# Two more U blocks per retrieval tile, thirty-six expert blocks on the spot, and one comparison for four one-hot rows

## The reference, cut to what matters

```
q = (xb @ wq).reshape(T, PEER_HEADS, 2, PEER_DKEY // 2)
s = jnp.einsum('thpk,hpnk->thpn', q, keys)
sv, si = lax.top_k(s, PEER_TOPK)                       # 16 of 128, per head and half
cand = sv[:, :, 0, :, None] + sv[:, :, 1, None, :]     # 16 x 16 sums
cv, ci = lax.top_k(cand, PEER_TOPK)
e = i1 * PEER_NKEYS + i2                               # 8 heads x 16 = 128 experts per token
gate = jax.nn.softmax(cv, axis=-1)
act = jax.nn.gelu(jnp.einsum('ted,td->te', u_tab[e], xb))
return jnp.einsum('te,ted->td', gate * act, v_tab[e])
```

## Time and profile before

| what | us |
|---|---|
| median of three runs | 4249.58 |
| lowest and highest run | 4244.55, 4253.15 |
| profiled execution | 4253.82 |
| its span, first to last instruction | 4252.2 |
| DVE busy in the span | 2870.1 (67%) |
| PE busy in the span | 3772.1 (89%) |

### The profile page before, as it was taken

One profiled execution on the slowest core, in us unless ns is written; L12 is line 12 of the kernel. 1 busy time (PEld: TensorE's weight loads), 2 busy tenths in 40 slices (PEclk: granted clock), 3 DMA queues, 4 the chain that ended last, 5 costly groups with the idle time before them and its releaser, 6 DMA issues. The chain is left out here.

```text
span 4252.2 us, 62663 instructions
## 1 busy us (share of the span) xinstructions
PE 3772.1 (89%) x21957; PEld 3272.0 (77%) x21957; DVE 2870.1 (67%) x7070; ACT 1065.8 (25%) x1921; POOL 1407.0 (33%) x1144
## 2 busy tenths in 40 slices
PE   4999899888798888888999899999999899999996
PEld 3999788876698888887888788887888566555665
DVE  3653334437211999999998599999999465555566
ACT  4443222224211222223333222222222111111112
POOL 0120244432100000000000355655564466666641
PEclk7999899999899999999999999999999999999998
DMA  4111211114221323333766688888887699999974
GB/s 160 35 47 47 76 49 56 65 44 155 102 90 47 122 96 113 108 98 110 184 173 179 232 306 311 312 312 304 312 308 268 267 376 380 361 366 358 375 287 156
DMA packets 464443, 823.68 MB, mean 194 GB/s; under 512 B 224352, under 2 KB 286048, under 8 KB 462432
## 3 DMA queue, kind: packets, MB, share of 16 engines
q0 software_dynamic: 120816, 444.13, 29.1%
q1 hardware_dynamic: 343408, 376.80, 26.4%
HBM read 708.89 MB, written 111.94 MB: 193 GB/s over the span
## 5 line engine op out<-in xcount | busy, mean ns | idle before, releaser
L2273 POOL DMA_INDIRECT stored_rows<-in_peer_v,peer_idx x384 | 398.0, 1036 | 117.7 <-issue 107.3
L2506 POOL DMA_INDIRECT peer_y<-in_peer_u_rows,experts_idxU x231 | 318.7, 1379 | 263.4 <-DVE peer_y L2595 182.3
L2385 PE MATMUL stored_pv<-peer_xh 128*128 128x512 f32 x912 | 374.1, 410 | 35.5 <-DVE peer_xl L2316 31.6
L1797 PE MATMUL topk_pu<-peer_xh,topk_Uh 128*128 128x384 f32 x864 | 303.0, 351 | 88.6 <-DVE topk_Ul L1784 88.6
L2386 PE MATMUL stored_pv<-peer_xl,peer_xh 128*128 128x512 f32 x912 | 359.3, 394 | 0.0
L2387 PE MATMUL stored_pv<-peer_xh,peer_xl 128*128 128x512 f32 x912 | 356.8, 391 | 0.0
L2339 DVE TENSOR_TENSOR peer_y<-peer_y,stored_pv 128x512 f32<-128x512 f32 x456 | 293.2, 682 | 44.5 <-PE stored_pv L2387 44.5
L2312 DVE TENSOR_TENSOR peer_xl<-stored_Vr,peer_xh 128x1024 fp32r<-128x1024 f32 x76 | 94.1, 1238 | 329.9 <-ACT peer_xh L2291 329.9
L2385 PEld LDWEIGHTS stored_pv<-peer_xh 128*128 128x128 f32 x912 | 171.8, 188 | 169.1 <-issue 55.8
L1798 PE MATMUL topk_pu<-peer_xl,topk_Uh 128*128 128x384 f32 x864 | 298.2, 345 | 0.0
L1799 PE MATMUL topk_pu<-peer_xh,topk_Ul 128*128 128x384 f32 x864 | 298.0, 345 | 0.0
(11 more groups left out here) (374 smaller groups left out, 9697.8 us busy)
## 6 DMA issues: line engine op xcount, KB each, us to landing
gates<-gates_G SPq DMA_DIRECT2D x48, 1024.0 KB, 11.3
stored_Vr<-in_peer_v SPq DMA_DIRECT2D x76, 512.0 KB
stored_C<-acts SPq DMA_DIRECT2D x76, 384.0 KB, 6.5
stored_G<-gates SPq DMA_DIRECT2D x76, 384.0 KB, 8.5
topk_Ur<-in_peer_u SPq DMA_DIRECT2D x56, 512.0 KB, 3.7
experts_Ur<-in_peer_u SPq DMA_DIRECT2D x52, 512.0 KB, 7.3
experts_Vr<-in_peer_v SPq DMA_DIRECT2D x52, 512.0 KB, 8.4
acts<-topk_act SPq DMA_DIRECT2D x108, 192.0 KB, 1.9
```

Source lines behind the costliest of these rows:

```text
L1797: mm(dst, self.Uh[slot][:, k, :], self.xh[:, k, cols], start=(k == 0), stop=False)
L2273: pool.indirect_dma_start(buffer(g, j), None, dram["peer_v"].rearrange("a b d -> (a b) d"), bass.IndirectOffsetOnAxis(idx[:, n:n + 1], 0)) ...
L2385: mm(pv[r % RING][:], Ch[p][j][:, t], Vh[p][j][:, cols], start=(j == 0), stop=False)
L2506: pool.indirect_dma_start(ug[i], None, dram["peer_u_rows"], bass.IndirectOffsetOnAxis(which, 0)).then_inc(ug_in[i], 16)
```

## The change

Retrieval makes eight U blocks per tile with a ring of four slots (72 instead of 54), the extra blocks behind the gates are two instead of four, so `MADE` is 92 instead of 76. The stage on the spot has 36 blocks (18 pairs instead of 26), the stored stage 92 (46 pairs instead of 38). `PER` becomes 23 instead of 16. In the gates one tensor_tensor of 128 x 512 makes the four `one` rows of a bank; the `scaled` rows stay as they are.

```diff
-TOPK_AHEAD, TOPK_RING = 6, 3
+TOPK_AHEAD, TOPK_RING = 8, 4
 GATE_AHEAD, GATE_RING = 3, 3
-EXTRA = 4
+EXTRA = 2
 MADE = TILES * TOPK_AHEAD + DENSE * GATE_AHEAD + EXTRA
...
                     dve.wait_ge(used, t * BANKS + (b + 1))
+                    four = core.slotT[:, 2, bass.ds(t * P + (FIRST + b * TG), TG)].unsqueeze(2).to_broadcast([P, TG, P])
+                    nc.vector.tensor_tensor(one[i][:], iota[:].unsqueeze(1).to_broadcast([P, TG, P]), four, ALU.is_equal)
                     for j in range(TG):
                         slot = lambda which: core.slotT[:, which, bass.ds(t * P + (FIRST + b * TG + j), 1)]
-                        nc.vector.tensor_scalar(one[i][:, j, :], iota[:], slot(2), None, ALU.is_equal)
                         last = nc.vector.tensor_scalar(scaled[i][:, j, :], iota[:], slot(1), slot(0), ALU.is_equal, ALU.mult)
                     last.then_inc(hot, 1)
```

## The result

The changed kernel takes 4346.94 us against 4251.24 before, a ratio of 1.0227 with a 95% interval of 1.0208 to 1.0245: slower by 96 us. The forecast was 64 us slower. The kernel before has four runs here, one more than in the table of before. All times are medians of runs at the usual granted clock of 0.94 to 0.97; one of the four runs of e6_extra0, 6333 us at a clock of 0.553, is left out.

The account below looks back on a forecast made before the run. Stages add, each with its own limit: DVE in retrieval, gates and on the spot, DMA in the first 32 stored pairs. 90 - 38 - 19 - 109 + 140 = +64 us gave 4314 us; own range 4290 to 4338, 8 in 10 4275 to 4355.

Parts of the forecast that it names:

- the rival in which the gates gain nothing: Gates: the comparison costs as much as four rows, or PE takes over; 4352 us in all, chance 5%.
- The signs: Profile after: DVE waits in retrieval 5.6 and 2 us, steps 46 to 49, gather waits 80 to 100, stored pairs 17.5.
- Retrieval, +90: Two more blocks per tile: DVE work 63.7 us plus waits of 2.1 and 5.6 make 71.4, times nine tiles.
- The upper bound of 72.9 us: Retrieval tile if each DVE wait costs PE as much again as the 1.5 us from its clock's 0.96; +103 us.
- Gates, -38: One comparison of 0.60 us replaces four rows of 0.80 us per bank, 6.4 us per tile, six tiles.
- extra blocks, -19: Behind the gates, two extra blocks instead of four end the stage 19 us earlier; bounds -16 to -19.
- On the spot, -109: Eight pairs fewer, all 384 dots in 17 steps: 811 instead of 920 us; bounds -175 to -37.
- the 4.9 us of waiting per step: On the spot: DVE's gather waits of 1.9 + 2.1 + 0.9 us, making a step 47.5 us.
- one turn of 9.9 us for all slots: On the spot: a gather slot's time from one dot to the next, 9.4 us in the trace, 9.9 with mean wait.
- gathers turn slower: On the spot: gather slots turn in 11.4 us under 23 dots, waits 9.4 a step; 4386 us, chance 6%.
- Stored, +140: Eight more pairs behind the 32 with gathers, at 17.5 us each; bounds 135 (PE alone) and 142.
- a pair leaves the stage on the spot for 13.6 us and enters another for 17.5: The forecast's stated loss: moving pairs to the stored stage costs more, while 18 blocks enter retrieval for 5 us each.

Follow-up runs that it names:

- e6_extra0: Kernel before with the one-hot comparison and no extra blocks behind the gates (28 pairs on the spot, 36 stored): 4211.36 us.
- The last comparison: Kernel before with comparison and eight gather slots (4170.95 us) beside the changed kernel with casts earlier, loads spread and eight slots (4220.46 us).
- e3_casts: Changed kernel with ACT's cast of U block n + 2, not n + 1, ahead of the gelus of block n in retrieval: 4313.62 us.
- e1_onehot: Kernel before with only the one-hot comparison in the gates, one tensor_tensor for four rows: 4211.09 us, ratio 0.9864.
- e2_rows: Changed kernel with the four old one-hot rows in place of the comparison, so the new split alone: 4386.91 us, ratio 1.0306.
- e8_all: Changed kernel with casts one block earlier, SP's loads spread over the step and eight gather slots: 4220.46 us, ratio 0.9916.
- e9_extra0_eight: Kernel before with the one-hot comparison, no extra blocks, spread loads and eight gather slots: 4156.17 us, ratio 0.9762, fastest of all.
- e10_onehot_eight: Kernel before with the one-hot comparison and eight gather slots, its old split of blocks kept: 4170.95 us, ratio 0.9795.
- e4_spread: Changed kernel with SP's load order on the spot altered: next U and both V blocks ahead of the second block's gates: 4299.14 us.

## Why the prediction was right, point by point

**The sign and the order of size.** Right: the sum had one large loss in retrieval that nothing gives back, and a trade between two stages at nearly equal prices. The last comparison shows that the split itself loses 48 us even with its waits mended. The measured 4346.94 us lies in the range for 8 in 10, 4275 to 4355, but outside the forecast's own 4290 to 4338; it is nearest to the rival in which the gates gain nothing (4352), which is not what happened. The signs came as named: DVE's waits for exp and for the cast, steps of 48.97 us (46 to 49), waits for gathers of 97.9 us (80 to 100), stored pairs of 17.2 us.

**Retrieval, +90 against +94.8.** Shown by e3_casts: the 4.1 us over PE's time hang on the cast behind the gelus of two blocks earlier. The tile is 72.2 us where 71.4 were forecast; the wait for exp was 2.83 instead of 2.1, since PE began block 6 later than I had it: DVE's subtract for it is done at 1943.86 (its start, 1942.72, and 1.14), but PE ends block 5 only at 1944.87, so that block stands in the way. The upper bound of 72.9 us took PE to lose more to its clock as DVE waits more, by 1.5 us that the rows shown do not give; the granted clock of the stage rose instead, from 0.96 to 0.98.

**Gates, -38 against -36.4, extra blocks, -19 against -19.8.** Shown by e1_onehot and e2_rows. The comparison costs 0.60 us from start to start, as taken. The page of the Trainium skill that spoke against the edit (VectorE: DVE Perf Modes, section "Why tensor_tensor can't do 2×_2P or 4×") did not decide it here: 512 elements by tensor_tensor take 0.60 us, four times 128 by tensor_scalar 0.80. By which part of these times the form decides, and by which the number of instructions, no run here shows.

**On the spot, -109 against -85.** The step that failed is the 4.9 us of waiting per step, worked out from one turn of 9.9 us for all slots. The work was right: 42.6 us per step without waits were forecast, and e8_all has 42.7. The waits were 97.9 / 16 = 6.1 us instead of 4.9, and sixteen steps of 48.97 instead of 47.5 are 23.5 us, nearly the stage's whole miss of 24. A turn has no one length. Where a dot waited, it was anything from 7.3 to 14.3 us, since a gather beside SP's loads lands after 10.2 us and the others after 5.8. The prediction had spread its 4.9 us over thirteen dots, one wait for each turn of the slots. In the trace 90.4 of the 97.9 us stand on three dots, the last three before a step's first coefficients, and the V loads are issued just ahead of them. So the forecast of 4.9 came as near as it did in part by luck. The trace of before could have told it: there too gathers beside the V loads took 10.0 us, and the median of 6.5 mixed them with the others. I had set bytes aside with a mean rate of 315 GB/s against 369; the burst runs at 407 to 415, at a busy share of 1.02. I had also taken PE's 883.9 busy us in this stage for overlapping records. PE's products take 33.0 us of a step (e9_extra0_eight) of 36.5, so it was nearly full before; with 18 pairs it does not matter. The rival "gathers turn slower" (11.4 us, 9.4 of waiting) had the direction right and the size too large.

**Stored, +140 against +144.7.** Eight pairs at the 17.2 us that the last twelve take in the mean are 138. The 7 us that are left are hardly more than what the stage differs by between runs with the same split (1011.2 to 1016.8 us). Whether V's load or PE sets the 17 us was not tried. In the trace the 72 products of a pair stand back to back for some 16.5 us, and PE then waits 0.2 to 1.1 us for DVE's last subtract, so the two are close.

**The one sentence that was wrong about the reason.** I wrote that a pair leaves the stage on the spot for 13.6 us and enters another for 17.5. 13.6 (109 / 8) was a price with waits in it. Without them a pair costs 17.0 there and 17.3 in the stored stage, and what the change loses is the retrieval (94.8 us) and the gathers' waits (49.4 more).

## What to carry to other kernels

Price a moved piece of work in each stage by what binds that stage after the move, and take the waits out before comparing: here the two prices were nearly equal, and only the fee for moving was left. Where a wait for a transfer is to be forecast, look at the DMA engines' share and at the transfers' times in the few microseconds of the wait, not at the stage's mean or median. Then the number of buffers is the cheap cure (43 us from e1_onehot to e10_onehot_eight); the order of the loads was one with 23 dots a step (50 us in e4_spread), and none with 15. A part that gains by itself (the comparison, 40 us) can be hidden in a change that loses; the parts are worth a run each.

## What the runs showed that I had not expected

One more gather slot at five saved 19 us of waiting, three more with the old split all 43: with eight slots the gathers keep up over a whole step, and the waits are a matter of rows in hand when the burst begins. And the same order of loads that halved the waits with 23 dots a step did nothing with 15 (63.1 against 57.9 us); one wait of 2.2 us became several of about 1.
